# Three outputs between preparation and scan, attention values one round later, and a projection's output ahead of the low-rank sums

## The reference

```python
def mla_qkv(p, prm, pos):
    q_a, kv_a, k_rope = jnp.split(p, [MLA_Q_RANK, MLA_Q_RANK + MLA_KV_RANK], axis=-1)
    q = (rmsnorm_2(q_a, prm['g_qa']) @ prm['w_q_up']).reshape(B, L, MLA_HEADS, MLA_QK)
    kv = (rmsnorm_2(kv_a, prm['g_kva']) @ prm['w_kv_up'])...
...
def latent_attention(q, k_lat, v_lat, k_ctx, v_ctx, scale):
        s = jnp.concatenate([s_ctx, s_lat], axis=-1).astype(jnp.float32) * scale
        p = jax.nn.softmax(s, axis=-1)
        return p[..., :n_ctx] @ v_ctx + p[..., n_ctx:] @ v_lat      # as einsums
...
def mixer_ab(hc, hl, row, col, need_ctx, prm):
    pc, pl = hc @ prm['w_in'], hl @ prm['w_in']
    r, v, dirs, g = rwkv_prep(p[..., :RW_COLS], prm)     # 15 column blocks of 128
    y_c, states_c = rwkv_scans(r_c, v_c, dirs_c, (zero, zero))
    y_l, _ = rwkv_scans(r_l, v_l, dirs_l, states_c)
    o_l = latent_attention(q_l, k_l, vm_l, k_c, vm_c, scale)
    out_l = jnp.concatenate([rwkv_out(y_l, ...), o_l], axis=-1) @ prm['w_out']
```

## Time and profile before

| | |
|---|---|
| median of 3 executions | 2590.62 us (2585.58 to 2597.38) |
| the profiled execution | 2596.23 us, its span 2594.4 us |
| mean granted TensorE clock | 0.962 |
| PE busy | 2379.0 us, 92% of the span |
| DVE busy | 1746.2 us, 67% |
| ACT busy | 1053.4 us, 41% |
| POOL busy | 343.0 us, 13% |

### The profile page before, as it was taken

The page is one execution under the profiler, slowest core; times in us unless marked ns, Lnnn a source line. Parts: engine busy times, 40 slices in busy tenths (PEclk is TensorE's granted clock), DMA queues, the critical chain, the costliest instruction groups (busy, mean ns, idle before and its releaser), DMA issues.

```text
span 2594.4 us, 38771 instructions
## 1 busy us (share of the span) xinstructions
PE 2379.0 (92%) x15040; PEld 1759.5 (68%) x15040; DVE 1746.2 (67%) x3348; ACT 1053.4 (41%) x2064; POOL 343.0 (13%) x534
## 2 busy tenths in 40 slices
PE   7999999799999799889998899988899998898997
PEld 3788888554888699833444577776576776667775
DVE  4875786576746778722657766665678885648985
ACT  4222222233221434421144244443467773446884
POOL 0111110100000011100200233331022210001220
PEclk9999999899999899999999999999999999998998
DMA  8555653231326478511010100000279993115995
GB/s 307 200 196 195 219 195 138 102 138 65 120 69 218 144 270 284 188 41 65 33 41 25 42 2 3 3 2 2 99 266 346 332 319 115 57 65 191 348 326 198
DMA packets 115063, 386.98 MB, mean 149 GB/s; under 512 B 20160, under 2 KB 22336, under 8 KB 114624
## 3 DMA queue, kind: packets, MB, share of 16 engines
q1 hardware_dynamic: 76640, 276.33, 30.3%
q0 software_dynamic: 34848, 95.47, 10.9%
q10 hardware_dynamic: 3392, 12.70, 1.3%
HBM read 389.66 MB, written 26.21 MB: 160 GB/s over the span
## 4 chain that ended last, share of the span: by engine, by line
PE 33%; DVE 14%; DMA 9%; ACT 6%; issue 3%; POOL 0%; DVEq 0%; ACTq 0%; SPq 0%; POOLq 0%
PE ps L143 32%; DMA RG<-in_w 6%; DVE moe0wl L152 2%; DVE moe1wl L152 2%; DMA AR<-in_a 1%; DVE rwMM L172 1%; PE ps L146 1%; DVE f2wl L152 1%; DVE acc L160 1%; ACT moe0wh L149 1%; ACT moe1wh L149 1%; DVE H L160 1%; ACT gqaas L149 1%; DVE rwXF L152 1%; ACT rwWU L149 1%
## 5 line engine op out<-in xcount | busy, mean ns | idle before, releaser
L143 PE MATMUL ps<-H,RG 128*128 128x256 f32 (+2 forms) x1088 | 363.9, 491 | 14.0 <-ACT H L149 14.0
L160 DVE SCALAR_TENSOR_TENSOR acc<-AR,cs,acc 128x512 f32<-128x512 f32 x420 | 295.9, 747 | 44.7 <-DMA AR<-in_a 42.4
L143 PEld LDWEIGHTS ps<-H,RG 128*128 128x128 f32 (+1 forms) x1088 | 206.8, 193 | 156.0 <-issue 139.7
L152 DVE TENSOR_TENSOR moe0wl<-RG,moe0wh 128x1024 fp32r<-128x1024 f32 x144 | 173.3, 1221 | 38.3 <-ACT moe0wh L149 30.0
L149 ACT ACTIVATE moe0wh<-RG 128x1024 fp32r<-128x1024 f32 x144 | 151.1, 1062 | 69.2 <-DMA RG<-in_w 44.4
L199 POOL DMA_DIRECT2D AR<-in_a x152 | 82.4, 542 | 713.2 <-DVE acc L160 520.3
L149 ACT ACTIVATE f1wh<-RG 128x1024 fp32r<-128x1024 f32 x66 | 69.8, 1061 | 228.1 <-PE ps L143 228.0
L152 DVE TENSOR_TENSOR moe1wl<-RG,moe1wh 128x1024 fp32r<-128x1024 f32 x120 | 144.4, 1220 | 25.2 <-ACT moe1wh L149 19.8
L143 PE MATMUL ps<-f1hh,f1wh 128*128 128x512 f32 x352 | 143.2, 407 | 4.8 <-DVE f1hl L152 4.8
L149 ACT ACTIVATE moe1wh<-RG 128x1024 fp32r<-128x1024 f32 x120 | 125.8, 1062 | 49.0 <-DMA RG<-in_w 29.6
L143 PE MATMUL ps<-f1hh,f1wl 128*128 128x512 f32 x352 | 140.4, 399 | 0.0
(11 more groups left out here) (634 smaller groups left out, 5791.4 us busy)
## 6 DMA issues: line engine op xcount, KB each, us to landing
RG<-in_w SPq DMA_DIRECT2D x525, 512.0 KB
AR<-in_a POOLq DMA_DIRECT2D x152, 512.0 KB, 3.7
moe0back<-moe_outs ACTq DMA_DIRECT2D x4, 1024.0 KB, 8.0
CT<-in_consts ACTq DMA_DIRECT2D x1, 2546.0 KB, 14.1
X<-in_x ACTq DMA_DIRECT2D x1, 2048.0 KB, 11.6
moe_rows<-moe0ht POOLq DMA_DIRECT2D x4, 512.0 KB, 5.2
moe1back<-moe_outs ACTq DMA_DIRECT2D x2, 1024.0 KB, 6.0
X<-in_ctx ACTq DMA_DIRECT2D x1, 1024.0 KB, 5.8
```

The source lines that it names most:

```text
L143: return Silent() if self.e is None else self.e.matmul(out, lhs, rhs, start=start, stop=stop, skip_group_check=True)
L152: return Silent() if self.e is None else self.e.tensor_tensor(out, a, b, op)
L160: return Silent() if self.e is None else self.e.scalar_tensor_tensor(out=out, in0=a, scalar=s, in1=b, op0=op0, op1=op1)
```

## The change

Three things, each a matter of order; no arithmetic changes.

1. `Attention.parts`: the product with the values comes one round later, in round 2p+5 for pair p where it was 2p+4, and every attention has one round more (`rounds`): 12 for the window attention, 20 for the other two. `Gqa.lead_pe` has an empty entry for that round. The added round also takes two more pieces of `Ada`'s work.
2. `Mla.pe`: RWKV output 0 goes ahead of the sums `nq`, output 1 between `nq` and `nk`; output 2 alone is left behind `nk`.
3. `Rwkv.pe` and `MixerAb`: outputs 1 to 3 of `out1` stand between preparation and scan, and outputs 4, 5, 6, 7 go into rounds 3, 4, 6, 8. The adds to `X` on DVE follow them; the keys and the bonus term on DVE begin 2 rounds later, the bonus on PE and its DVE part 4 rounds later.

```diff
--- before.py
+++ after.py
@@ -1508,11 +1508,11 @@
     def parts(self, u):
 
         inside = lambda r: r if 0 <= r < 2 * self.n else None
-        pair = u - self.LAG - 2
+        pair = u - self.LAG - 3
         return inside(u), inside(u - 1), inside(u - self.LAG), pair // 2 if pair >= 0 and pair % 2 == 0 else None
 
     def rounds(self):
-        return range(2 * self.n + self.LAG + 1)
+        return range(2 * self.n + self.LAG + 2)
 
     def pe(self, e, needs, beside=None, turned=None, values=()):
 
@@ -2233,10 +2233,10 @@
             e.wait_ge(*tok)
         pe_tiles(g, e, ps[64:96, :], [W("ab_w_in_2", k, 2560, ix, 32) for k in range(KT)], lambda k: g.H[:, k, :]).then_inc(*p.up("kr"))
         g.ws.settle("mla kr", p.now())
+        rw.output_pe(e, 0)
         self.nq.pe(e)
-        rw.output_pe(e, 0)
+        rw.output_pe(e, 1)
         self.nk.pe(e)
-        rw.output_pe(e, 1)
         rw.output_pe(e, 2)
         e.wait_ge(*S.dve.at("ka scaled"))
         for h in range(8):
@@ -2543,7 +2543,7 @@
             for f in range(4):
                 ins = e.transpose(ps[:, f * P:(f + 1) * P], self.V[:, f, tb * P:(tb + 1) * P], g.C("ident"))
             ins.then_inc(*p.up(("vk", tb)))
-        beside(e, 1, 5)
+        beside(e, 1, 4)
         S.meet(e, p, "prep")
         self.run(e, self.unit_pe, self.close_pe, amid)
         S.meet(e, p)
@@ -3005,7 +3005,7 @@
         self.g, self.ada, self.pre, self.router = g, ada, pre, router
         S = self.S = Step(g, "ab")
         SO = self.SO = Step(g, "abo")
-        self.amid = [0, 2, 4]
+        self.amid = [3, 4, 6, 8]
         with ExitStack() as s1:
             R = g.sb(s1, "abr", [P, 4, T])
             with ExitStack() as s2:
@@ -3031,9 +3031,9 @@
     def amid_pe(self, e, r):
 
         if r in self.amid:
-            self.out1.one_pe(e, self.amid.index(r) + 5)
-        if 6 <= r < 14 and r % 2 == 0:
-            self.rwkv.bonus_pe(e, r // 2 - 3)
+            self.out1.one_pe(e, self.amid.index(r) + 4)
+        if 10 <= r < 18 and r % 2 == 0:
+            self.rwkv.bonus_pe(e, r // 2 - 5)
         self.late_pe(e, r)
 
     def late_pe(self, e, r):
@@ -3072,14 +3072,14 @@
         self.out1.one_dve(e, 0)
 
     def amid_dve(self, e, r):
-        for f in (1, 2, 3) if r == 0 else (4,) if r == 2 else ():
+        for f in (1, 2) if r == 0 else (3,) if r == 2 else ():
             self.out1.one_dve(e, f)
         if r - 1 in self.amid:
-            self.out1.one_dve(e, self.amid.index(r - 1) + 5)
-        if 4 <= r < 12:
-            (self.rwkv.bonus_term_dve if r % 2 else self.rwkv.keys_dve)(e, r // 2 - 2)
-        if 7 <= r < 15 and r % 2:
-            self.rwkv.bonus_dve(e, r // 2 - 3)
+            self.out1.one_dve(e, self.amid.index(r - 1) + 4)
+        if 6 <= r < 14:
+            (self.rwkv.bonus_term_dve if r % 2 else self.rwkv.keys_dve)(e, r // 2 - 3)
+        if 11 <= r < 19 and r % 2:
+            self.rwkv.bonus_dve(e, r // 2 - 5)
         self.late_dve(e, r)
 
     def pe(self, e):
@@ -3279,7 +3279,7 @@
             self.router.pe(e, 1)
             self.lead = [self.out.bank(e, f) for f in range(2)]
             self.tiles = [[g.ws.tile(s[:4], s[4], s[5]) for s in self.out.specs(f)] for f in range(2)]
-        for k in {first: range(0, 4), first + 1: range(4, 6), first + 2: range(6, 7)}[u]:
+        for k in {first: range(0, 4), first + 1: range(4, 6), first + 2: range(6, 7), first + 3: ()}[u]:
             self.led_pe(e, k)
 
     def led_pe(self, e, k):
```

## The result

The changed kernel takes 2565.07 us (median of 4 executions, 2561.08 to 2570.34) against 2592.13 for the kernel before in the same comparison: a ratio of 0.9896, interval 0.9870 to 0.9923. That is 27 us faster where 17.8 was forecast; 2565 lies inside the range of 2561 to 2586. A second comparison gave 0.9899 (0.9865 to 0.9933). The forecast case is the one that came, but most of its terms had another size, and one that was costed at nothing is among the largest.

A forecast was written before the change was run, and what follows sets the result against it. PE was taken as the largest part of the chain (33%), with idle and half-clock time to recover. Gains 6.4 + 4.1 + 4.2 + 0.8 + 2.3 = 17.8 us, from the median 2590.6 to 2572.8 us; range 2561 to 2586.

The forecast's parts named there:

- Part 1: Low-rank sums: an RWKV output moved ahead covers PE's 4.81 us wait and restores the clock; 6.4 us gained.
- the 1.30 stays: Low-rank sums: PE's second wait, 1.30 us before the sums of KA, was to remain unchanged.
- The narrow cover: Behind the second sums: one output (6.95 us) still covers DVE's scaling of KA, by about 1.3 us; 0.2 deducted.
- MLA attention: Values one round later: four PE waits for `rwa` go, 3.8 us, plus 0.3 at the end; 4.1 us gained.
- GQA attention: Values one round later: 2.7 us at the start, 1.8 over four cycles, less 0.3 at the tail; 4.2 gained.
- 2 x 3.11 plus 0.42 for that copy: GQA attention: DVE sets the two-round cycle at 6.64 us, so each of four cycles gains 0.46 us.
- Window attention: Values one round later: the one product's wait of 0.83 us goes; 0.8 us gained.
- Ada's pieces: Window attention's added round: two pieces, 2.73 us on DVE, ahead of scan preparation; costed at nothing, at most 2.7 lost.
- The scan's start: RWKV scan: outputs cover the first POOL wait and DVE waits, 2.3 us, less 0.5, plus 0.5 for clock; 2.3 gained.
- the rival paced by the unit's chain: Scan's start: no wait goes and adds to X lengthen the chain, 4 us lost; total 2579.1 us, chance 0.12.
- the waits only move: Attentions: DVE or ACT sets the round, only the window attention's 0.8 us is saved; total 2581.1 us, chance 0.16.
- The slow one: Scan's start at half clock for 60 us loses 30 us; total 2605.1 us, chance 0.06.

The follow-up runs named there:

- the third part alone: Only the scan-start edits in `Rwkv.pe` and `MixerAb` (three outputs ahead, four in its rounds), against the kernel before: ratio 0.9990 (0.9971 to 1.0009).
- the second part alone: Only the product with the values one round later, in all three attentions, against the kernel before: ratio 0.9943 (0.9922 to 0.9965).
- the kernel before once more: The kernel before the change, profiled again without any edit: one execution took 2587.21 us.

## Why the prediction came out as it did

- **Part 1, forecast 6.4, measured 7.4.** The wait and the clock were right. The step that failed is "the 1.30 stays": it fell to 0.52, because I asked what releases the square (DVE's scaling) and not what else stands in ACT's queue ahead of it. The narrow cover held; that it is a cover, and of 7.6 us, the run without it shows.
- **MLA attention, 4.1 against 6.1.** The bank as the cause is shown by the run that empties it earlier (4.1; the forecast had 3.8). What was short is the rest, where I counted 0.3: the waits at the end fell from 2.2 (1.6, and 0.6 for `abom`) to 1.0, and each projection, now behind transposes and not behind the product, takes 7.03 and not 7.13.
- **GQA attention, 4.2 against 6.1** between the first two profiles (5.8 of the means, since one of the old order had its first product at full clock). Of this 2.6 came at the start (2.7 forecast), as DVE's rows have it. The step that failed is "2 x 3.11 plus 0.42 for that copy": it took a round's length for DVE's work, where part of it was a wait for ACT. The two runs with the copy doubled and moved show that the first copy is free. The steady cycles gave 0.89 each and not 0.46, and they were five and not four; two waits of 0.53 at the end cost 1.0 and not 0.3.
- **Window attention, 0.8 against 2.2 of the means.** The 0.83 is gone. In the two profiles without half clock there (the third part alone, the second part alone) the stretch is 88.2 and 86.4 us, 1.8 apart, 0.5 of it a shorter wait for ACT's `hgk`. The rest is not located.
- **Ada's pieces, forecast "nothing, at most 2.7 lost"; the stage that they left became 6.6 shorter.** This is the largest error, and it was one of direction: I looked for what the moved work would disturb where it goes, and not for what it frees where it leaves. It left a stage where PE waits for DVE. That the stage is shorter rests on fourteen profiles; that the pieces are the reason rests on DVE's smaller count and on the shorter waits for DVE, which are 3.3 of the 6.6, and is argued. No run kept these two pieces in their old stage beside the new order of the attention, and the other 3.2, PE's shorter busy time, has no cause that a run shows.
- **The scan's start, 2.3 against 1.3 of the means, and for another reason.** "Outputs of 3.5 stand about the first POOL wait (1.1) and the DVE ones" failed: outputs 4 and 5 stand ahead of the matmul on whose result POOL waits, so the wait stays, as in the rival paced by the unit's chain, and those for DVE stay too, but for 0.3. The waits that went, 2.0 for POOL and 1.6 for ACT, were not in the sum, and the new one for `abv` gave back 1.4 of them. The 3.5 that the adds to X should cost in that rival did not show: the start is shorter and not longer. What the new order gains is that the scan hangs less on when PE is through with its outputs. The new order took 43.1 to 43.3 in every profile, the old one 43.2 to 45.0. A low clock in the scan's rounds is not all of that: the two profiles of the old order that have it took 44.9, but two at 1.00 throughout took 44.5 and 45.0. The one at 43.2, the run that empties the bank earlier, differs from them ahead of the outputs, where PE's last matmuls of the preparation took 10.96 us and not 12.31 (the first row is from that run, the second from the kernel before once more):

```profile
1404.30 10.96 PE L143 MATMUL ps<-rwa,RG 64*128 64x512 f32 x14 [1.83 <-ACT rwscr L149]
```

```profile
1408.98 12.31 PE L143 MATMUL ps<-rwa,RG 64*128 64x512 f32 x14 [1.83 <-ACT rwscr L149]
```

- **The rivals.** That the waits only move was wrong for both attentions. The slow one, the scan at half clock, did not come: the windows above are at 1.00. On the rule of the Trainium skill, page "TensorE: Matmul & The Clock Gate", section "A second HAM failure mode: psum-queue depth-cycling", that frequent short idle times make the clock swing: in the GQA rounds the clock was 1.00 with waits of 0.99 and is so without. Behind the single waits of 3.1 and 5.6 us that two runs added, PE was at half clock for a while. Two groups of the first block's scan, behind waits of 0.81, ran at either level from execution to execution: the half-clock ones agree with the rule, the others had the same waits.

The total gain is 27.1 where 17.8 was forecast, 9.3 more. By the means of the stages, part 1 brings 1.0 of it, the MLA attention 2.0, GQA 1.6, the window attention 1.4, the second feed-forward 6.6, and the scan's start takes 1.0: 11.6, which is 2.3 more than the 9.3 and within what the medians can tell. That the total came within 10 us of the forecast is in part luck: the sum had no term for the stage with the largest surplus, and the other terms were off by 1 to 2 us each.

## What to carry to other kernels

When work moves, price both ends: the engine it leaves may be the one that others wait for. A round's length read off a trace is no engine's work; look for the gaps in it before adding an operation to it. And a filler covers a wait only if it stands between the two instructions of the chain, not ahead of both.

## What the runs showed of the hardware

The same kernel ran the same two groups of 16 matmuls in 3.79 us or in 2.05, with the same waits before them, from one execution to the next; the first experts' layer varied from 343.3 to 354.2 us over fourteen profiles, while the MLA attention in one order repeated to 0.03 us. 21 executions of the kernel before spread over 2579.43 to 2601.74 us. So for a change of 1 to 2 us the stage in the profile is the instrument, and the total is not.
